# High parts of two norms' columns: from VectorE's cast to a second activation on ScalarE

## The reference

```
def _standardize(x):
    mu = mean(x); var = mean((x - mu)**2)
    return (x - mu) * rsqrt(var + LN_EPS)

h = _standardize(x) * (1.0 + sc1) + sh1        # "norm 2" of the kernel
mix = hybrid_mixer(h, ...)                     # starts with h @ w_in
x = layer_norm(ALPHA * x + (1.0 + g1) * mix, ...)
h = _standardize(x) * (1.0 + sc2) + sh2        # "norm 3" of the kernel
f = conv_glu_ffn(h, ...)                       # starts with h @ w_ffn_up
```

## Time and profile before

| | us |
|---|---|
| median of 3 runs | 1468.87 |
| lowest, highest | 1467.88, 1471.39 |
| profiled execution, its own time | 1466.43 |
| its span, first to last instruction | 1464.6 |
| TensorE busy | 1417.5 |
| VectorE busy | 854.4 |
| ScalarE busy | 589.6 |
| gpsimd busy | 678.3 |

### The profile page before, as it was taken

How to read it: one execution, slowest core, us unless ns; L and a number is a source line. 1 busy time by engine, 2 the same in 40 slices (tenths; PEclk the granted TensorE clock), 3 DMA queues, 4 the chain that set the end, 5 groups by cost and what they waited for, 6 DMA issues and landing times.

```text
span 1464.6 us, 19070 instructions
## 1 busy us (share of the span) xinstructions
PE 1417.5 (97%) x7074; PEld 1148.3 (78%) x7074; DVE 854.4 (58%) x1440; ACT 589.6 (40%) x786; POOL 678.3 (46%) x516
## 2 busy tenths in 40 slices
PE   5999999999999999999999999999979999999997
PEld 4877866778888888887888877888868888888886
DVE  3547367549667888986672565356675333332257
ACT  5566467352222221225344665543353322331231
POOL 3533445436556555653452334355524544545453
PEclk9999999999999999999999999999989999999999
DMA  7432300235647464232854433354322232232221
GB/s 289 152 111 82 121 24 2 73 112 184 233 159 244 158 204 156 86 115 101 122 185 131 164 126 127 122 209 149 109 99 88 86 115 86 87 115 86 89 92 79
DMA packets 50693, 185.79 MB, mean 127 GB/s; under 512 B 15088, under 2 KB 16496, under 8 KB 35888
## 3 DMA queue, kind: packets, MB, share of 16 engines
q1 hardware_dynamic: 43120, 170.99, 34.7%
q10 hardware_dynamic: 7488, 13.63, 2.6%
HBM read 169.79 MB, written 12.59 MB: 125 GB/s over the span
## 4 chain that ended last, share of the span: by engine, by line
PE 79%; DVE 4%; ACT 1%; issue 1%; POOL 0%; DVEq 0%; ACTq 0%
PE bank L452 16%; PE bank L454 16%; PE bank L453 16%; PE bank L502 8%; PE bank L504 8%; PE bank L503 8%; PE bank L476 1%; PE bank L918 1%; PE bank L790 1%; PE bank L947 1%; DVE Alo L1701 1%; PE bank L693 1%; PE bank L891 1%; PE bank L884 0%; DVE X L2466 0%
## 5 line engine op out<-in xcount | busy, mean ns | idle before, releaser
L1558 POOL TENSOR_TENSOR wlo<-raw,whi 128x512 fp32r<-128x512 f32 x424 | 610.0, 1469 | 652.4 <-ACT whi L1030 652.3
L452 PE MATMUL bank<-Ahi,whi 128*128 128x512 f32 x1024 | 406.4, 397 | 6.3 <-DVEq L1656 3.5
L454 PE MATMUL bank<-Ahi,wlo 128*128 128x512 f32 x1024 | 400.9, 391 | 0.0
L453 PE MATMUL bank<-Alo,whi 128*128 128x512 f32 x1024 | 400.7, 391 | 0.0
L1030 ACT ACTIVATE whi<-raw 128x2048 fp32r<-128x2048 f32 x111 | 212.7, 1916 | 229.1 <-PE bank L504 204.7
L452 PEld LDWEIGHTS bank<-Ahi,whi 128*128 128x128 f32 x1024 | 193.6, 189 | 50.9 <-issue 7.0
L454 PEld LDWEIGHTS bank<-Ahi,wlo 128*128 128x128 f32 x1024 | 193.4, 189 | 41.1
L453 PEld LDWEIGHTS bank<-Alo,whi 128*128 128x128 f32 x1024 | 193.6, 189 | 39.8 <-issue 0.7
L502 PE MATMUL bank<-whi,Bhi 128*128 128x512 f32 x496 | 193.2, 389 | 1.1 <-DVEq L1938 1.1
L504 PE MATMUL bank<-whi,Blo 128*128 128x512 f32 x496 | 193.0, 389 | 0.0
L503 PE MATMUL bank<-wlo,Bhi 128*128 128x512 f32 x496 | 192.9, 389 | 0.0
(11 more groups left out here) (404 smaller groups left out, 1925.2 us busy)
## 6 DMA issues: line engine op xcount, KB each, us to landing
raw<-in_ws SPq DMA_DIRECT2D x112, 1024.0 KB, 4.9
adaw<-in_ada SPq DMA_DIRECT2D x48, 512.0 KB, 4.7
spill<-stage ACTq DMA_DIRECT2D x32, 256.0 KB, 2.2
X<-in_x SPq DMA_DIRECT2D x8, 512.0 KB, 6.7
gates<-spill SPq DMA_DIRECT2D x16, 256.0 KB, 5.4
w1k<-in_w1k SPq DMA_DIRECT2D x1, 2048.0 KB, 15.4
w1v<-in_w1v SPq DMA_DIRECT2D x1, 2048.0 KB, 10.8
XM<-spill ACTq DMA_DIRECT2D x8, 256.0 KB, 3.2
```

The costliest lines, as they stand in the source:

```text
L452: pe.matmul(ps[:], wh, hi[:, k], start=(k == 0), stop=False)
L453: pe.matmul(ps[:], wh, lo[:, k], start=False, stop=False)
L454: ins = pe.matmul(ps[:], wl, hi[:, k], start=False, stop=(k == kn - 1))
L1558: pool.tensor_tensor(wlo[slot][:, part], raw[slot][:, part], rd(whi[slot][:, part]), ALU.subtract).then_inc(sem("lo_split"), 1)
```

## The change

In norms 2 and 3 `scaled` issues two activations for each column on the same bank: the same scale and bias, once into `FN` (fp32) and once into `Ahi` (rounded to fp32r by the write). The bank's release moves to the second one. On VectorE the cast is gone; the subtraction into `Alo` remains and counts `A_ready`. Norms 0 and 1, the other users of `split_to`, and TensorE's, POOL's and SP's programs are as before.

```
                     else:
                         m = (s - 2) * 24 + k
-                        act.activation(FN[s][k][:], ps[:], ACT.Identity, scale=mod[:, m + 8:m + 9],
-                                       bias=mod[:, m:m + 1]).then_inc(taken(n)[0], 1)
+                        for part in (FN[s][k][:], Ahi[:, k]):
+                            ins = act.activation(part, ps[:], ACT.Identity, scale=mod[:, m + 8:m + 9],
+                                                 bias=mod[:, m:m + 1])
+                        ins.then_inc(taken(n)[0], 1)
...
                     else:
                         dve.wait_ge(*taken(n))
-                        split_to(Ahi[:, k], Alo[:, k], FN[s][k][:], "A_ready")
+                        tt(Alo[:, k], FN[s][k][:], rd(Ahi[:, k]), ALU.subtract).then_inc(sem("A_ready"), 1)
+                        dve.wait_ge(sem("A_ready"), v.did("A_ready"))
```

## The result

| | before | after |
|---|---|---|
| median of 20 runs each, us | 1468.90 | 1472.54 |
| lowest, highest | 1466.02, 1472.41 | 1468.70, 1474.68 |
| profiled execution, span | 1466.43, 1464.6 | 1472.98, 1471.2 |
| mean granted clock | 0.992 | 0.988 |

The ratio is 1.0019 with a 95% interval of 1.0010 to 1.0027, so 1.5 to 4.0 us slower. The forecast was 1471.0 (1467.4 to 1473.0), 0.15% slower; the measured median is in the range, 1.5 us above the forecast. The forecast called the loss not measurable; with 20 runs a side it can be told from none.

What follows compares the result with a forecast made beforehand. TensorE's stream of matmuls plus its holes was taken as the bound. Norm 2's start +0.65, its clock +1.6 and norm 3 -0.1 gave +2.15 us on 1468.87: 1471.0 us, range 1467.4 to 1473.0.

Steps and rivals of the forecast that it cites:

- The start in norm 2: TensorE's pair of products in norm 2 waits for column 1's bank, released by the fourth activation: +0.65 us.
- Column 0's low part: In norm 2, VectorE's first subtraction is done 0.5 us before the fourth activation's end, so it is not the last wait.
- ScalarE's pace: Norm 2's activations start 0.667 us apart, 1.33 us a column against TensorE's 1.38, so nothing starves after the start.
- Rival (c): Norm 2: activations on one bank do not overlap, 0.79 us apart, so ScalarE bounds: 1472.1 us; chance 8%.
- The clock in norm 2: The longer hole ahead of norm 2's pair brings one stretch of 3.4 us at 1.2 GHz: +1.6 us.
- Rival (a): The clock stays at its upper level in norm 2, leaving 0.65 - 0.1: 1469.4 us; chance 26%.
- rival (d): Longer holes in norms 2 and 3 bring longer stretches at 1.2 GHz: 1474.3 us, +0.37%; chance 7%.
- Norm 3: Later start costs 0.33 us, the stall ahead of the last column goes, 0.41 us: -0.1 us, other end +0.24.
- The weight tiles: Weight tiles behind norms 2 and 3 come later but stay covered, by 4.7 and 2 us: no cost.
- Rival (e): The weight tile comes late after norm 3, about 0.5 us: 1471.5 us; chance 5%.
- The sum: Start and clock in norm 2 plus norm 3, 0.65 + 1.6 - 0.1: +2.15 us, +0.15%; chance 42%.
- Rival (b): The pair's start follows column 0's low part, not the bank, so freed VectorE wins: -0.27 us, 1468.6 us; chance 12%.

Runs made afterwards that it cites:

- the kernel with norm 3 alone: Against the kernel before, only norm 3 reads its banks twice on ScalarE; norm 2 keeps its cast on VectorE: ratio 1.0005 (0.9994 to 1.0015).
- the repeat: The changed kernel run once more, nothing further edited, against the kernel before: ratio 1.0014 (1.0003 to 1.0025).
- the kernel with the late bank: TensorE's pair of products waits for its second bank only ahead of the second product: ratio to before 0.9988 on the changed kernel, 0.9982 on the one before.
- the kernel with both findings: Against the kernel before: columns 0 and 1 cast on VectorE, 2 to 7 read twice, second bank asked for late: 0.9973 (0.9964 to 0.9981), median 1465.11 us.

## Why the prediction was right, point by point

- **The start in norm 2** was to be 0.60 to 0.76 us later because of column 1's bank. It was 0.71 in all five profiles with two readings ahead of the release and the old taking of the banks, the wait is named in the rows, and the late asking for the bank took 0.50 back. Shown.
- **Column 0's low part** was to be done 0.5 us ahead of that. It was done at 675.98 against 676.53. Shown.
- **ScalarE's pace** was to be 0.667 us; it is 0.66 to 0.67, two readings of one bank included. Rival (c), with 0.79, fell. The estimate of 0.71 us from the Trainium skill's page "ScalarE: Activation LUTs", section "What ACT_TABLE_LOAD costs", is 0.04 too high here; the trace decides.
- **The clock in norm 2** was the one large term, +1.6 us. The profile shows it: the pair takes 12.7 us for 11.1. But the step was put too simply, as if 1.62 us kept the clock and 2.3 lowered it. With 1.62 us idle, and nothing filled, it fell in 2 of 6 profiles: in the kernel with norm 3 alone and in the one with the first two columns cast and the late bank. With 2.33 us it fell in 5 of 5, and once with 1.83. Norm 1 says the same: behind 1.81 us it fell in 10 of 10 profiles, behind 0.97 us in none of 4. So a median moves by part of 1.6 us: by these counts some 1.1 us, an estimate. The runs bear it out. By each run's mean granted clock, the four kernels of the experiments with the hole of 2.33 us were at the lower level 1.2 to 4.0 us longer than the kernel before beside them, 2.4 us on average; at 1.6 us for 3.4 that is 1.1 us as well. Rival (a), clock kept, was not seen with the long hole. Nor was rival (d), longer stretches: it was one stretch of 3.4 us in norm 2 each time, and 10.2 us around norm 3 as before. Its premise misread: the granted clock was already 0.50 from 1087.4 to 1090.6, inside the hole of 4.33 us and not only behind it.
- **Norm 3** was put at -0.1 us, with +0.24 as the other end. The stall went as described (last subtraction 0.69 us). The piece from the last turns to the next product took 16.45 or 16.46 us in four profiles of the old form, and 16.3, 16.9, 16.1 and 16.2 in the four of the new one, 0.1 less on average. The sign is left open, and my upper end was too low: it reached +0.5. What I did not see is why only the new form scatters. In the old form VectorE's last subtraction begins 13.08 or 13.09 us behind the last turns in all four and ends the piece, whether 4.1 or 5.4 us of the pair ran at the lower level. In the new form nothing holds the last column back, so the clock shows: with 3.3, 3.4, 3.7 and 5.0 us of the pair at the lower level the piece took 16.1, 16.2, 16.3 and 16.9 us.
- **The weight tiles** were to cost nothing. In the first profile after, TensorE waited 0.76 us for `wlo` at 747.7, where ScalarE had waited 7.5 us for a transfer (4.0 in before). In the other four profiles with all of norm 2's banks read twice it did not. It is not a steady cost; that the change never has a share in it isn't shown. Rival (e), a late weight tile behind norm 3, shows in no profile of the new form.
- **The sum** was +2.15 us; the ratio gives 2.8 (1.5 to 4.0), and the repeat 2.1 (0.4 to 3.7). From the profiles the terms are 0.71 + 1.1 - 0.1 = 1.7 us, so about 1 us of the 2.8 is not assigned, though 1.7 is within both intervals. That 2.15 came out near is in part luck: the clock's 1.6 was counted in full, as if no run of the kernel before paid it and every run after did.
- **Rival (b)**, start behind the low part, fell with the rows above; the kernel with the late bank shows what it would look like.

## What to carry to other kernels

Splitting work from a busy engine to an idler one pays where it makes the hand-over that the bottleneck waits for come sooner. Here that was a PSUM bank's release, and it came later. The question to ask is which release the next product needs first, and how many instructions now stand ahead of it. A list of resources taken at the head of a stage should be asked for one by one, each where it is first used: on the kernel before, this alone gave 0.18%, about as much as the change cost. And a slow stretch costs nothing where TensorE has nothing to do, or where another engine's last result ends the stage anyway (norm 3 in the old form), so its length isn't what it costs.

## What was unexpected of the hardware

Two executions of one program enter norm 2 up to 1.7 us apart, and kernels with the same code ahead of it 3.9 us apart; extra stretches at the lower clock near 22, 110, 141 and 196 us go with it. The profile of the kernel with both findings was even the slowest of its 12 runs (1469.13 us, median 1465.11). A single profile against another can't resolve a change of 3 us; laying the same-numbered matmuls of both side by side and reading only the piece from the edit on could.
